# Attention scores from rounded halves in three passes, and the low halves of the attention stage subtracted in pieces

## The reference

```
q, kc, vc, ks, vs, kw, vw, gates, z = split(h @ w_in)      # q scaled by 64 ** -0.5
k_cmp, v_cmp = compress(kc), compress(vc)                  # 31 compressed positions
p_c = softmax(q . k_cmp - slope * distance)                # branch 0, compressed
p_s = softmax(q . ks    - slope * distance)                # branch 1, selected blocks
p_w = softmax(q . kw    - slope * distance)                # branch 2, window of 512
o = gate0 * p_c @ v_cmp + gate1 * p_s @ vs + gate2 * p_w @ vw
out = (o * silu(z)) @ w_out
```

## Time and profile before

| | us |
|---|---|
| median of three runs | 1929.93 |
| the profiled execution's own time | 1929.67 |
| its span (first to last instruction) | 1927.9 |
| PE busy | 1910.2 (99%) |
| PE weight loads busy | 1514.0 (79%) |
| DVE busy | 1151.1 (60%) |
| POOL busy | 795.5 (41%) |
| ACT busy | 577.0 (30%) |

### The profile page before, as it was taken

How to read it: one execution, slowest core, us unless ns; L and a number is a source line. 1 busy time by engine, 2 the same in 40 slices (tenths; PEclk the granted TensorE clock), 3 DMA queues, 4 the chain that set the end, 5 groups by cost and what they waited for, 6 DMA issues and landing times.

```text
span 1927.9 us, 26511 instructions
## 1 busy us (share of the span) xinstructions
PE 1910.2 (99%) x9852; PEld 1514.0 (79%) x9852; DVE 1151.1 (60%) x2085; ACT 577.0 (30%) x1117; POOL 795.5 (41%) x454
## 2 busy tenths in 40 slices
PE   9999999999999999999999999999999999999999
PEld 6977777788888876777788888888788888888887
DVE  6789998788974546676654444333654564444311
ACT  3146655316731143444221111101422221111000
POOL 3632222378754432222344444444233344444443
PEclk9999999999999999999999999999999999999999
DMA  6511110222122231111232222322122222222332
GB/s 214 181 66 34 34 45 23 97 85 93 45 77 98 95 118 55 55 66 55 70 111 98 97 93 94 108 102 96 66 77 77 75 91 98 98 96 92 112 115 77
DMA packets 54916, 167.72 MB, mean 87 GB/s; under 512 B 6896, under 2 KB 14960, under 8 KB 54688
## 3 DMA queue, kind: packets, MB, share of 16 engines
q1 hardware_dynamic: 47488, 155.90, 23.8%
q10 hardware_dynamic: 7328, 10.47, 2.0%
HBM read 157.96 MB, written 2.10 MB: 83 GB/s over the span
## 4 chain that ended last, share of the span: by engine, by line
PE 89%; DVE 8%; issue 2%; ACT 1%; DMA 0%; ACTq 0%; POOL 0%; DVEq 0%
PE bank L189 18%; PE bank L193 18%; PE bank L190 18%; PE bank L592 5%; PE bank L597 5%; PE bank L593 5%; DVE prob L1663 2%; DVE ssb L1650 2%; PE bank L1288 1%; PE bank L1313 1%; PE bank L209 1%; PE bank L2648 1%; PE bank L2637 1%; PE bank L206 1%; PE bank L203 1%
## 5 line engine op out<-in xcount | busy, mean ns | idle before, releaser
L172 POOL TENSOR_TENSOR wlo<-raw,whi 128x1024 fp32r<-128x1024 f32 x248 | 595.0, 2399 | 887.0 <-DVE whi L180 887.0
L180 DVE CAST whi<-raw 128x1024 fp32r<-128x1024 f32 x288 | 208.0, 722 | 331.5 <-PE bank L193 240.9
L189 PE MATMUL bank<-xh,whi 128*128 128x512 f32 x888 | 347.6, 391 | 0.2 <-DVE xl L373 0.2
L190 PE MATMUL bank<-xl,whi 128*128 128x512 f32 x888 | 345.8, 389 | 0.0
L193 PE MATMUL bank<-xh,wlo 128*128 128x512 f32 x888 | 220.5, 391 | 0.0
L189 PEld LDWEIGHTS bank<-xh,whi 128*128 128x128 f32 x888 | 166.8, 188 | 38.8 <-issue 2.9
L193 PEld LDWEIGHTS bank<-xh,wlo 128*128 128x128 f32 x888 | 167.7, 189 | 35.0
L190 PEld LDWEIGHTS bank<-xl,whi 128*128 128x128 f32 x888 | 166.9, 188 | 34.8 <-issue 0.5
L592 PE MATMUL bank<-xh,whi 128*128 128x512 f32 x424 | 175.2, 413 | 0.0
L593 PE MATMUL bank<-xl,whi 128*128 128x512 f32 x424 | 166.0, 392 | 0.0
L189 PE MATMUL bank<-ghi,whi 128*128 128x512 f32 x308 | 119.8, 389 | 0.0
(11 more groups left out here) (430 smaller groups left out, 3467.9 us busy)
## 6 DMA issues: line engine op xcount, KB each, us to landing
raw<-in_weights_dram SPq DMA_DIRECT2D x288, 512.0 KB, 3.2
h<-in_x_dram SPq DMA_DIRECT2D x4, 512.0 KB, 6.5
out_dram<-h ACTq DMA_DIRECT2D x8, 256.0 KB, 2.0
etab<-in_even_tables_dram ACTq DMA_DIRECT2D x1, 1730.0 KB, 6.5
sz<-su SPq DMA_DIRECT2D x16, 64.0 KB, 2.0
sz<-su SPq DMA_DIRECT2D x16, 48.0 KB, 2.0
x_kh<-kvc_h ACTq DMA_DIRECT2D x2, 256.0 KB, 5.0
x_kl<-kvc_l ACTq DMA_DIRECT2D x2, 256.0 KB, 6.8
```

What stands on the lines that cost most here:

```text
L172: nc.gpsimd.tensor_tensor(wlo[:, s % 2, :], raw[:, s, :], whi[:, s % 2, :].bitcast(F32), ALU.subtract).then_inc(w_lo, 1)
L180: nc.vector.tensor_copy(whi[:, t_of_4 % 2, :], raw[:, t_of_4, :]).then_inc(w_hi, 1)
L189: nc.tensor.matmul(to, w_h[k], rhs_hi(k), start=first and k == 0, stop=False)
L190: nc.tensor.matmul(to, w_h[k], rhs_lo(k), start=False, stop=False)
```

## The change

The keys ks and kw are kept as two rounded halves: DVE writes the scaled product to `sq`, ACT rounds it into `nk` (now float32r), POOL subtracts (`pool_keys_low`) into four new tiles `nkl` that lie where early buffers were. In POOL's list these four come between the subtractions of weight tiles 6 to 9. DVE's scaling for u = 6 and 7 waits for the halves of two tiles earlier.

The queries get a second ACT instruction: `qst` takes the rounded ones, `sq` the full ones. POOL subtracts in two pieces (`query`) into the last chunk of `nh` and `nl`. The compressed scores read `sq` and stay float32.

`pe_scores` runs three passes (high by high, low by high, high by low), each a float32r matmul for either head, added up in PSUM, in place of one float32 matmul for either head.

POOL's subtractions in the attention stage are cut: `low` into four pieces of 256 columns, `rest` into two. `query(i + 1)` stands ahead of `low(7 + 2i)`.

```diff
@@ -1060,12 +1060,12 @@
         used[0] = work
         kvc = [at(f"kvc_{part}", [P, 4, S], F32R) for part in "hl"]
         used[0] = work
-        qst = at("qst", [P, 2, S])
+        qst = at("qst", [P, 2, S], F32R)
         dist = at("dist", [P, 2, 2, S])
         ssb = at("ssb", [P, 2, 2, S])
         prob = at("prob", [P, 2, 2, S])
         probt = at("probt", [P, 2, 2, S])
-        nk = at("nk", [P, 4, S])
+        nk = at("nk", [P, 4, S], F32R)
         ntab = at("ntab", [P, S + 3 * P + 16])
         dist_t, cdist_t = ntab[:, 0:S], ntab[:, S:S + P]
         cmask = ntab[:, S + P:S + 2 * P].rearrange("p (b n) -> p b n", n=NW)
@@ -1084,12 +1084,21 @@
         cpt = at("cpt", [2 * NW, S])
         stat = at("stat", [P, 12])
         nmix = at("nmix", [P, S])
+        after_nmix = used[0]
+        SSQ_AT = base - 4 * S
+        LNV_AT = SSQ_AT - 4 * 32 - 8 * S
+        XF_AT = LNV_AT - 8 * S
+        nkl = [at(f"nkl{u}", [P, S], F32R, offset=offset)
+               for u, offset in enumerate((XF_AT, XF_AT + 4 * S, LNV_AT, SSQ_AT))]
+        used[0] = after_nmix
+        qlow = (nh[:, KC - 1, :], nl[:, KC - 1, :])
         n_loaded = sem("n_loaded")
         n_gmm = sem("n_gmm")
         n_gs = sem("n_gs")
         n_zero = sem("n_zero")
         n_kvh = sem("n_kvh")
         n_kvl = sem("n_kvl")
+        n_kl = sem("n_kl")
         n_wgate = sem("n_wgate")
         n_x2 = sem("n_x2")
         n_cb = sem("n_cb")
@@ -1195,6 +1204,8 @@
             pe.wait_ge(n_cb, 4 + 4)
             pe.wait_ge(acc_free[0], freed(O0["nsa_rest"] + 4))
             pe_cmp_scores(pe, 0, bank[6])
+            pe.wait_ge(n_kvh, 8)
+            pe.wait_ge(n_kl, 4 + 1)
             pe_scores(pe, 0)
             pe_beside(pe, 0, 1)
             pe_beside(pe, 1, 0)
@@ -1264,7 +1275,7 @@
         def pe_cmp_scores(pe, i, to):
 
             for qb in range(QB):
-                mm = nc.tensor.matmul(to[:, qb * 2 * NW:(qb + 1) * 2 * NW], qst[:, i % 2, qb * P:(qb + 1) * P],
+                mm = nc.tensor.matmul(to[:, qb * 2 * NW:(qb + 1) * 2 * NW], sq[:, i % 2, qb * P:(qb + 1) * P],
                                       kcb[:, i // 4, :, :].rearrange("p h n -> p (h n)"), start=True, stop=True)
             mm.then_inc(n_cs, 1)
 
@@ -1283,10 +1294,13 @@
             for br in range(2):
                 if M:
                     pe.wait_ge(n_m, 4 * (M - 1) + 2 * br + 2)
-                for hd in range(2):
-                    b = 64 * hd
-                    mm = nc.tensor.matmul(bank[2 + 2 * br + hd][:, 0:w], qst[b:b + 64, i % 2, qb * P:(qb + 1) * P],
-                                          nk[b:b + 64, 2 * br + j, 0:w], start=True, stop=True)
+                q_h, q_l = (x[:, qb * P:(qb + 1) * P] for x in (qst[:, i % 2, :], qlow[i % 2]))
+                k_h, k_l = (x[:, 0:w] for x in (nk[:, 2 * br + j, :], nkl[2 * br + j][:]))
+                for n, (q, k) in enumerate(((q_h, k_h), (q_l, k_h), (q_h, k_l))):
+                    for hd in range(2):
+                        b = 64 * hd
+                        mm = nc.tensor.matmul(bank[2 + 2 * br + hd][:, 0:w], q[b:b + 64], k[b:b + 64],
+                                              start=n == 0, stop=n == 2)
                 mm.then_inc(n_s, 1)
 
         def pe_turn(pe, M, br):
@@ -1323,6 +1337,7 @@
             if M < LAST:
                 if m == 3:
                     pe.wait_ge(n_c, 4 * (i + 1) + 2)
+                    pe.wait_ge(n_kl, 4 + i + 2)
                 if m == 0 and i:
                     pe.wait_ge(n_cta, i + 1)
                 pe_scores(pe, M + 1)
@@ -1372,7 +1387,8 @@
         def act_nsa(act):
             def high(u):
                 act.wait_ge(acc_free[u % 2], freed(O0["nsa_kv"] + u))
-                nc.scalar.activation(kvc[0][:, u, :], bank[4 + u % 2], ACT.Copy).then_inc(n_kvh, 1)
+                to, of = (kvc[0][:, u, :], bank[4 + u % 2]) if u < 4 else (nk[:, u - 4, :], sq[:, u % 2, :])
+                nc.scalar.activation(to, of, ACT.Copy).then_inc(n_kvh, 1)
 
             def windows(kv):
                 act.wait_ge(n_kvl, 2 * kv + 2)
@@ -1404,6 +1420,8 @@
             nc.scalar.activation(gsig[:].rearrange("p b g -> p (b g)"), bank[3][:, 0:4 * 48], ACT.Sigmoid).then_inc(n_gs, 1)
             high(3)
             windows(1)
+            for u in range(4, 8):
+                high(u)
             for k in range(4):
                 scaled_high(k)
             hidden(0)
@@ -1414,6 +1432,7 @@
             scaled_high(7)
             hidden(2)
             hidden(3)
+            act.wait_ge(n_kl, 4)
             act_take_turned(act, "nsa_rest", 0, 4, nin, 0)
             act_nsa_q(act, 0)
             act.wait_ge(n_c2, 1)
@@ -1441,7 +1460,8 @@
             act.wait_ge(tile_done, T0["nsa_rest"] + r + 1)
             if i >= 2:
                 act.wait_ge(n_s, 8 * (i - 1))
-            nc.scalar.activation(qst[:, i % 2, :], acc[0][:], ACT.Copy, scale=0.125).then_inc(acc_free[r % 2], 1)
+            nc.scalar.activation(qst[:, i % 2, :], acc[0][:], ACT.Copy, scale=0.125).then_inc(n_kvh, 1)
+            nc.scalar.activation(sq[:, i % 2, :], acc[0][:], ACT.Copy, scale=0.125).then_inc(acc_free[r % 2], 1)
 
         def act_nsa_z(act, i):
 
@@ -1544,7 +1564,10 @@
                 if 2 <= u < 4:
                     dve.wait_ge(n_kvh, u - 1)
                     dve.wait_ge(n_kvl, u - 1)
-                nc.vector.tensor_tensor(bank[4 + u % 2] if u < 4 else nk[:, u - 4, :], acc[u % 2][:], rstd[:],
+                if u >= 6:
+                    dve.wait_ge(n_kvh, u - 1)
+                    dve.wait_ge(n_kl, u - 5)
+                nc.vector.tensor_tensor(bank[4 + u % 2] if u < 4 else sq[:, u % 2, :], acc[u % 2][:], rstd[:],
                                         ALU.mult).then_inc(acc_free[u % 2], 1)
                 if u == 0:
                     nc.vector.tensor_tensor(nmix[0:48, :], bank[2][0:48, :], rstd[0:48, :], ALU.mult).then_inc(n_gmm, 1)
@@ -1702,14 +1725,22 @@
             if M < LAST:
                 dve_scale(dve, M + 1, 0)
 
+        def pool_keys_low(pool, u):
+
+            pool.wait_ge(n_kvh, u + 1)
+            nc.gpsimd.tensor_tensor(nkl[u - 4][:], sq[:, u % 2, :], nk[:, u - 4, :].bitcast(F32), ALU.subtract).then_inc(n_kl, 1)
+
         def pool_nsa(pool):
 
             t0 = T0["nsa_rest"]
 
             def low(r):
                 pool.wait_ge(w_hi, t0 + r + 1)
-                nc.gpsimd.tensor_tensor(wlo[:, r % 2, :], raw[:, r % 4, :], whi[:, r % 2, :].bitcast(F32),
-                                        ALU.subtract).then_inc(w_lo, 1)
+                for first in range(0, SLAB, 2 * P):
+                    part = slice(first, first + 2 * P)
+                    sub = nc.gpsimd.tensor_tensor(wlo[:, r % 2, part], raw[:, r % 4, part], whi[:, r % 2, part].bitcast(F32),
+                                                  ALU.subtract)
+                sub.then_inc(w_lo, 1)
 
             def slope(i):
                 if i == 0:
@@ -1722,10 +1753,22 @@
 
             def rest(i):
                 pool.wait_ge(n_hi, i + 1)
-                nc.gpsimd.tensor_tensor(nl[:, i, :], nmix[:], nh[:, i, :].bitcast(F32), ALU.subtract).then_inc(n_lo, 1)
+                for part in (slice(0, 2 * P), slice(2 * P, S)):
+                    sub = nc.gpsimd.tensor_tensor(nl[:, i, part], nmix[:, part], nh[:, i, part].bitcast(F32), ALU.subtract)
+                sub.then_inc(n_lo, 1)
+
+            def query(i):
+                r = 3 + 2 * i if i else 4
+                pool.wait_ge(n_kvh, 8 + i + 1)
+                pool.wait_ge(acc_free[r % 2], freed(O0["nsa_rest"] + r))
+                for part in (slice(0, 2 * P), slice(2 * P, S)):
+                    sub = nc.gpsimd.tensor_tensor(qlow[i % 2][:, part], sq[:, i % 2, part], qst[:, i % 2, part].bitcast(F32),
+                                                  ALU.subtract)
+                sub.then_inc(n_kl, 1)
 
             for r in range(6):
                 low(r)
+            query(0)
             slope(0)
             for i in range(PAIRS):
                 if i < PAIRS - 1:
@@ -1734,6 +1777,7 @@
                 if i:
                     rest(i - 1)
                 if i < PAIRS - 1:
+                    query(i + 1)
                     low(7 + 2 * i)
             low(20)
             low(21)
@@ -2877,7 +2921,11 @@
         def _(pool):
             if "s5_in" in names:
                 pool_zeros(pool)
-                pool_stream(pool, 0, T0["nsa_rest"])
+                pool_stream(pool, 0, 6)
+                for u in range(4, 8):
+                    pool_low(pool, u + 2)
+                    pool_keys_low(pool, u)
+                pool_stream(pool, 10, T0["nsa_rest"])
                 pool_nsa(pool)
                 first = T0["nsa_out"] + 2
             else:
```

## The result

| | before | after |
|---|---|---|
| median, us | 1929.85 (1929.65 to 1930.02, 5 runs) | 1940.46 (1940.24 to 1941.51, 5 runs) |
| ratio | | 1.0056 (95% interval 1.0045 to 1.0067) |
| profiled execution, us | 1929.67 (span 1927.9) | 1941.14 (span 1939.4) |
| mean granted clock | 0.999 | 0.989 |

The forecast was 1928.0 us, with a range of 1923.8 to 1932.0. The change is slower by far more than the 0.2% that can be told apart.

What follows compares the result with a forecast made beforehand. The prediction took PE as the bound for most of an attention pair, with the chain through DVE in macro m = 2. It summed -3.1 - 2.7 - 0.8 + 0.3 + 1.5 + 3.0 = -1.8 us to 1928.0 us, range 1923.8 to 1932.0.

Steps and rivals of the forecast that it cites:

- the keys' low halves: In nsa_kv, four POOL subtractions stall DVE's small operations and PE waits for its cast: 3.0 us lost (0 to 4.5).
- the further stall: In the cmp stage, the fourth keys' subtraction holds up the DVE cast that was at 67.03, for another 0.9 us.
- the first rival: In nsa_kv, DVE's cast slips ahead of POOL and the keys' halves don't reach PE: 1925.1 us; 28%.
- The forecast's own sign for this term: The cmp stage ends 2 to 3.5 us later than at 89.0; an end at 89 would be wrong.
- The scores: Attention, three float32r passes for one float32 matmul: 0.44 us gained a pair, 3.1 us in all (0.3 to 5.0).
- those two rivals: In the scores: heads no longer side by side, about 1957 us, 7%; loads open in short passes, about 1943, 3%.
- The idle time before the turn: Attention, PE's 0.43 us idle a pair ahead of the compressed probabilities' turn, from DVE's m = 2 stall: 2.7 us gained.
- The start of the attention: POOL's distances and next weight tile, pushed back 3.3 us, meet DVE's first softmax: 1.5 us lost (0.3 to 2.5).
- The second copy of the first query: Start of the attention: the first query needs 2 x 0.7 us, hidden under PE's own work.
- The last pair and `rest`: Last pair's DVE stall falls from 2.05 to about 1.3: 0.8 us gained; the last `rest` in two pieces costs 0.3.

Runs made afterwards that it cites:

- e8: The change with twenty idle matmuls of 512 columns on PE ahead of the fifth cmp tile; 1938.69 us, ratio 1.0046.
- e3: The change with seven idle matmuls of 512 columns on PE ahead of the second cmp tile; median 1938.7 us, three of ten executions at 1928.4.
- e5: The change with idle matmuls of 512 columns on PE, seven ahead of the second cmp tile and five ahead of the third; 1929.01 us.
- e4: The kernel before with only POOL's subtractions of the attention stage cut in pieces as in the change; 1929.04 us, ratio 0.9996.
- e6: The change with keys' subtractions moved to the attention's start and DVE's scaling of compressed probabilities between its two pairs of maxima; 1923.0 us.
- e7: e6 with POOL making the second pair's distances first and starting weight tile 6 only after DVE scaled the first probabilities; 1922.17 us.
- e9: The change with the keys' subtractions moved to the attention's start and POOL's instructions left whole; 1926.93 us, ratio 0.9985.
- e2: The kernel before with four idle POOL subtractions where the change has the keys'; 1943.6 us, ratio 1.0075.
- e10: e2 with only its second and third idle subtraction; 1931.36 us, nine of twelve executions at 1930.8 to 1931.7, three at 1942.5 to 1943.5.

## Why the prediction was wrong

**The step that failed is the keys' low halves.** Its mechanism was right and its sizes nearly so: the cast of the second cmp tile was put at 65.9 to 66.5 and came at 65.49 (in e8, the same instructions up to there, at 66.14), PE's wait at 1.6 to 2.3 us and it was 1.56 (in e8 2.00), the further stall at 0.9 and e3 shows 0.40 of it behind a filled first one. In the trace of after the cast at 52.69 did get ahead of POOL, as the first rival had it, but the operations behind it did not. The term was +3.0 us, and the runs with a full clock give 2.7 (e3) to 3.4 (e5). What failed is that the wait was priced as its own length, with a bound of 4.5. It also took the clock to half for 41 us, some 12 us more, and no rival had that. With e3's numbers the sum is 1928.0 - 0.3 + 12.1 = 1939.8 for 1940.46. The forecast's own sign for this term, a cmp stage that ends 2 to 3.5 us later than at 89.0, failed most plainly: it ended at 102.2.

That wait could have been given a second price. The earlier trace rows show the cmp stage on short matmuls, gapless, with 0.42 us of slack. And the trace of before holds one fall of the clock, in a later block, without any wait of PE. Its timeline and the busy times behind it:

```profile
1348.97 3.70 PE L1849 MATMUL bank<-gas,walpha 48*128 48x512 f32 x8
```

```profile
1352.60:1355.80 3.20, 3.20 (x9) 2.53 (x9) 3.13 (x5) 2.62 (x5) 0.00 (x0) 0.50 0.00 0
```

Behind eight matmuls of 48 rows the clock is at half, and under matmuls of 128 rows and 512 columns it is back 3.4 us later (the trace of after has the same place at full clock). So a rival "the clock falls" had a row to stand on: a thin stretch on PE was enough there, and a wait among short matmuls could be another. No row of before gave its chance in the cmp stage; its price could be bounded as short matmuls at half clock for the rest of the stage.

**The scores: right, and a little too small.** The twelve records of a macro in the chain of after, for 512, 128, 256 and 384 columns:

```profile
266.80 1.58 PE bank L1302 x12
...
274.96 0.81 PE bank L1302 x12
283.19 0.90 PE bank L1302 x12
289.11 1.25 PE bank L1302 x12
```

Forecast 1.59, 0.87, 0.96 and 1.27. The sum is 4.54; in before it is 1.92 + 0.65 + 1.06 and, in its chain, 1.49 for 384 columns:

```profile
304.77 1.49 PE bank L1288 x8
```

That makes 5.12, so the gain is 0.58 a pair for 0.44, and six pairs of it are the 3.5 us of the ledger. Both heads run side by side and the loads are hidden (at 128 columns the pairs of records start 0.11 us apart, inside the forecast's 0.08 to 0.13), so those two rivals fall.

**The idle time before the turn: wrong.** I took 2.7 us for it, from DVE's stall in m = 2. The scalings did fall to 0.87 us, as forecast, but the wait stayed. The chain of after:

```profile
275.78 0.60 PE bank L1315 x4
...
276.40 0.06 DVE probt L1694
...
277.01 0.28 DVE ssb L1673
...
277.93 0.34 DVE cst L1649
...
278.74 0.43 DVE cpr L1659
279.31 0.60 PE bank L1286 x4
```

It is a round trip: PE's transposes release DVE's copy at 276.40, and behind the copy in DVE's list stand four maxima and four small operations, to 278.74 + 0.43. PE, earlier by the scores' gain, only makes DVE's copy earlier; the length of the trip stays. DVE's timeline of after even has it idle before the copy:

```profile
276.40 0.69 DVE L1694 COPY probt<-bank 128x512 f32<-128x512 f32 x1 [0.38 <-PE bank L1315]
```

In before DVE does come to this copy without idle time, since its stall is still there:

```profile
291.91 0.68 DVE L1671 COPY probt<-bank 128x512 f32<-128x512 f32 x1
```

But the copy starts 0.70 us behind PE's transposes (291.21) and the turn (294.81) 2.90 behind the copy, and in after it is 0.69 (from 275.71) and 2.91: without the stall DVE only gets to wait for PE, and the trip is as long. In e4, where just the stall is shorter, DVE waits 0.23 us for PE there, and the pair stays. I had seen DVE 26.72 of 29.0 us busy and taken its stall for the cause. e6 shows what the trip costs: 0.37 us in each pair (28.04 for 28.41), gone by a change of order.

**The start of the attention**: +1.3 for 1.5, by the mechanism named: the pieces that run from 138.63 to 141.6 meet DVE's first softmax, and PE waits 1.28 us; in e7, where they come later, 0.39. The second copy of the first query, which the forecast took as free, is the 0.3 us ahead of the compressed scores. **The first to the second turn**: 1.2 gained, of which 0.58 is a pair's gain in scores. For the other 0.65 the runs leave two causes. The pieces alone bring it in the kernel before (e4 has 22.94 us there, 126.43 to 149.37, for 23.60), but e9, without pieces, has 22.39 as well; there `query` ahead of the weight tile in POOL's list is left, and no run takes that alone. **The last pair and `rest`**: 0.8 gained in all. The forecast had 0.8 for the stall, -0.3 for `rest` and some 0.3 of scores left in that stretch; POOL's last `rest` takes 1.42 us in two pieces for 1.28.

Without the fall the forecast would have held, in part by luck. The attention gave 4.2 us for 4.8, though the 2.7 didn't come: 1.3 more from the scores, 0.65 ahead of the second turn and 0.2 at the first stand against them. With 2.7 for the keys that makes 1929.85 - 4.2 + 2.7 = 1928.35, and e3's three executions at full clock have 1928.4. The range had one small slip: half the widths of its terms, squared and added, give 3.8 us and not 3.6.

## What to carry to other kernels

A wait that a change adds on PE among short matmuls is to be priced twice: by its length, and by what the work behind it costs at half the clock, for as long as that work is made of short matmuls. Not every wait has the second price (the one of 1.28 us at the first turn left the clock at full), so it belongs in the forecast as a rival with a chance. Look for the stages where PE is gapless with thin slack and put no POOL instruction beside a DVE chain there. When a kernel is slower and no engine's busy time tells why, the granted clock by stretch comes first. An engine that is nearly full isn't thereby the late one: read what the operation that releases PE waited for itself, since a round trip between two engines is shortened by the order of what is queued inside it, not by removing stalls elsewhere.

## What the hardware did that was not expected

- Waits of PE of 1.56 us (after), 0.89 us (e2) and 2.00 us (e8) in the cmp stage each went with a fall to half the clock, for 41, 37.5 and, up to the burst, 17 us. It came 0.8 us into the first wait and 0.5 and 1.2 us after the end of the others, so the wait's length alone doesn't say when. With 0.18 us the clock stayed full in the profiled execution, and it fell in 3 of 12 by their mean clocks (e10). What exactly decides it no run here shows.
- A wait of 1.28 us at the first turn of after left the clock at full, with PE busy for 3.26 of 5.00 us from 142 to 147. And in before it fell at 1352.6, at the end of eight matmuls of 48 rows, without a wait. One and the same kernel has executions 10 to 13 us apart by this (e3, e10).
- Back-to-back matmuls of 160 columns at half clock, PE busy for 39.8 of 40 us, did not bring the full clock back; twenty of 512 columns did within 6.48 us (e8).
- At half clock a matmul of 160 columns with its load starts every 0.21 us for 0.14, and not twice as far apart, as those of 512 columns nearly do (0.42 for 0.23).
- float32r matmuls of 64 rows and 128 columns, two heads side by side, start 0.11 us apart; DVE operations of 32 columns were blocked through two POOL instructions in a row, 3.24 us for 0.42.
